# Meta values in four column groups, a reordered last expert, and one activation table for both kinds of head

## What is computed

```python
# first block: 16 meta tokens stand before the 256, so L = 272
xn = rmsnorm(h, norm_mix_g)
sq, sk, sv, dq, dk, dv = split(xn @ w_in)          # 8 heads each
# stick-breaking head (width 128), causal
z = q @ k.T * 128**-0.5
u = where(causal, log_sigmoid(-z), 0)
a = where(causal, exp(log_sigmoid(z) + reverse_cumsum(u) - u), 0);  o = a @ v
# differential head: two softmaxes (width 64 each) with a distance bias
w = p[0] - lam * p[1];  o = rmsnorm(w @ v) * 0.8
h = h + (g0 * (o_sb @ w_br_sb) + g1 * (o_df @ w_br_df)) @ w_out
h = h + swiglu(rmsnorm(h))                          # width 2816
# second block: retention and dilated attention, then 32 experts, 4 a token
u = xb @ w1[e] + b1[e];  a = clamped_swiglu(u);  y += gate * (a @ w2[e] + b2[e])
out = rms_norm(h + modulation * y) * g_final
```

## Time and profile before

| | |
|---|---|
| median of 3 runs | 1876.97 us (1876.14 to 1877.78) |
| profiled execution | 1878.5 us, its span (first to last instruction) 1876.5 us |
| PE busy | 1807.3 us, 96% |
| DVE busy | 816.2 us, 43% |
| ACT busy | 532.4 us, 28% |
| DMA | 568.86 MB, mean 303 GB/s |
| L1136, low parts of the first block's weights | 88 on DVE, 1223 ns each |
| L2181 and L2222, products of the experts | 2048 and 1024 passes on PE, about 595 ns each |

### The profile page before, as it was taken

The page is one execution under the profiler, slowest core; times in us unless marked ns, Lnnn a source line. Parts: engine busy times, 40 slices in busy tenths (PEclk is TensorE's granted clock), DMA queues, the critical chain, the costliest instruction groups (busy, mean ns, idle before and its releaser), DMA issues.

```text
span 1876.5 us, 27470 instructions
## 1 busy us (share of the span) xinstructions
PE 1807.3 (96%) x11187; PEld 1221.8 (65%) x11188; DVE 816.2 (43%) x1363; ACT 532.4 (28%) x860; POOL 39.4 (2%) x65
## 2 busy tenths in 40 slices
PE   7999999999998999999999999999999999999996
PEld 6888889999997899899843443443443434434342
DVE  5445667788884544547522331232221322223222
ACT  5666666434433444455300000000000000000001
POOL 2000000000000000000000000000000000000000
PEclk9999999999997999999999999999999999999998
DMA  7333346778782744435999999999999999999994
GB/s 249 110 111 113 117 131 230 242 234 275 271 309 75 245 159 153 157 127 172 328 428 427 429 426 429 430 427 428 430 427 428 429 428 428 429 429 428 428 429 181
DMA packets 147898, 568.86 MB, mean 303 GB/s; under 512 B 6064, under 2 KB 102424, under 8 KB 123120
## 3 DMA queue, kind: packets, MB, share of 16 engines
q1 hardware_dynamic: 139616, 536.60, 72.5%
q0 software_dynamic: 8208, 31.20, 4.7%
HBM read 566.71 MB, written 3.43 MB: 304 GB/s over the span
## 4 chain that ended last, share of the span: by engine, by line
PE 75%; DMA 18%; DVE 3%; ACT 3%; issue 1%; SPq 0%; DVEq 0%; ACTq 0%
DMA s_ring<-in_w_mlp 17%; PE banks L2181 16%; PE banks L1756 9%; PE banks L2222 9%; PE banks L1758 8%; PE banks L1757 8%; PE banks L2192 4%; PE banks L1911 3%; PE banks L1912 3%; PE banks L1913 3%; PE banks L2165 2%; PE banks L1714 1%; PE banks L1777 1%; DMA s_ring<-in_w_ada 1%; PE banks L2200 1%
## 5 line engine op out<-in xcount | busy, mean ns | idle before, releaser
L2181 PE MATMUL banks<-s_ring,s_W 128*64 128x512 f32 x1568 | 351.6, 596 | 16.9 <-DMA s_ring<-in_w_mlp 15.9
L2181 PEld LDWEIGHTS banks<-s_ring,s_W 128*64 128x64 f32 x1568 | 107.0, 137 | 245.0 <-issue 201.8
L1072 ACT ACTIVATE s_W<-s_W 128x512 f32<-128x512 f32 x32 | 20.1, 630 | 759.7 <-DVE s_W L1624 759.7
L1616 DVE TENSOR_TENSOR s_W<-banks,s_W 128x512 f32<-128x512 f32 x32 | 22.1, 692 | 429.2 <-PE banks L2222 429.2
L2222 PE MATMUL banks<-s_ring,s_W 128*64 128x512 f32 x736 | 161.8, 592 | 0.0
L1366 DVE TENSOR_TENSOR r_w2l<-s_ring,r_w2h 128x1024 fp32r<-128x1024 f32 x96 | 117.3, 1224 | 89.1 <-ACT r_w2h L921 88.9
L1136 DVE TENSOR_TENSOR r_w2l<-s_ring,r_w2h 128x1024 fp32r<-128x1024 f32 x88 | 107.5, 1223 | 92.1 <-ACT r_w2h L737 91.9
L1598 DVE TENSOR_TENSOR s_W<-banks,s_W 128x512 f32<-128x512 f32 x128 | 82.2, 684 | 139.1 <-PE banks L2165 139.1
L1756 PE MATMUL banks<-r_x2h,r_w2h 128*128 128x256 f32 x448 | 131.0, 292 | 5.2 <-DVE r_x2l L1382 5.2
L2192 PEld LDWEIGHTS banks<-s_W 128*128 128x128 f32 x1024 | 116.7, 192 | 24.4 <-issue 24.4
L1758 PE MATMUL banks<-r_x2h,r_w2l 128*128 128x256 f32 x448 | 127.7, 285 | 0.0
(11 more groups left out here) (433 smaller groups left out, 3387.0 us busy)
## 6 DMA issues: line engine op xcount, KB each, us to landing
s_ring<-in_w_mlp SPq DMA_DIRECT2D x144, 2048.0 KB, 30.8
s_W<-in_w_mlp SPq DMA_DIRECT2D x48, 2048.0 KB, 31.0
s_ring<-in_w_in SPq DMA_DIRECT2D x62, 1024.0 KB, 5.1
s_ring<-in_w_ada POOLq DMA_DIRECT2D x24, 1024.0 KB, 9.0
s_ring<-in_w_ffn_gate SPq DMA_DIRECT2D x11, 1024.0 KB, 5.5
s_ring<-in_w_ffn_up SPq DMA_DIRECT2D x11, 1024.0 KB, 10.6
s_ring<-in_w_ffn_down SPq DMA_DIRECT2D x5, 2048.0 KB, 10.2
s_ring<-in_w_gate SPq DMA_DIRECT2D x8, 1024.0 KB, 5.7
```

The lines of the kernel that those rows point to most:

```text
L2181: last = mm(pb[b][64 * h:64 * h + 64, :], XgT[:, 2 * c + k, :], piece(n, 2)[:, k, 1024 * h + 512 * b:1024 * h + 512 * b + 512], start=Fals ...
```

## The change

**Meta values.** xm becomes plain float32: the 16 tokens and 16 columns of zeros. Eight float32 products of the raw weights, one for each block k, go to four groups of 32 output rows (k % 4), so that bank rows 0 to 127 hold four partial sums with zeros between; nothing adds them up but the heads' own products, which now run over all 128 rows (sv[:, 2], dv[:, 2], la, wT), with wvM holding the meta weights eight times. The group moves from the value piece's four units to the start of the unit ahead of it (units 7, 19, 31 and 43). Since DVE overwrites the raw weights, low1 of the piece's first unit waits for the group, and DVE does the low parts of the piece's first three units in that slot (lows1).

**Full rows.** ntriM is 128 rows, zero but for the first 16. L1832, L1844, L1883, L1870 and L1871 lose their narrow shapes.

**Table.** load_log_exp moves from differential head 0 to the start, behind the square root of the token norms.

**Last expert.** The pieces of expert 31 come in the order up 0 to 3, down 0, 1 of expert 30, and then the two of expert 31, the last one in two transfers with semaphores of their own. PE does the four up pieces in a row, the down pieces, with the transposes of expert 31's activation between the two; the last scatter goes to banks 0 and 1. g_final is spread ahead of the last expert and kept in SBUF by ACT (gfin). ACT squares each half of acc when it is complete.

```diff
-GR1, GR2 = group_list(PIECES1), group_list(PIECES2)
 V_KINDS = ("sv", "dv", "rv", "av")
+def meta_first(groups):
+    out = []
+    for x in groups:
+        if x[1] in V_KINDS and x[2] == 0:
+            out.insert(len(out) - 1, x)
+        else:
+            out.append(x)
+    return out
+GR1, GR2 = meta_first(group_list(PIECES1)), group_list(PIECES2)
...
+LAST = (0, 1, 4, 5, 2, 3)
...
+META_OF = {}
+for _n in range(3, len(UNITS1), 4):
+    if PIECES1[_n // 4][0] in V_KINDS:
+        META_OF[_n - 3] = UNITS1[_n].pop(0)
+        UNITS1[_n - 4].insert(0, META_OF[_n - 3])
+def lows1(h):
+    if h + 1 in META_OF:
+        return [h + 1, h + 2, h + 3]
+    return [] if h + 2 in META_OF or h + 3 in META_OF else [h + 3]
...
-    xm = rounded("xm", False, 23168, KT, 2 * M)
+    xm = area(W, 23168, KT, 2 * M)
...
-    skM, ntriM, wvM = area(W, 20864, HEADS, P), W[0:M, 21888:22016], area(W, 22016, 2, 2 * M)
+    skM, ntriM, wvM = area(W, 20864, HEADS, P), W[:, 21888:22016], area(W, 22016, 2, P)
...
+    gfin = W[:, 10368:11392]
...
-        "sc_mm", "acc_done",
-        "over_in", "over_pe", "over_act", "over_dve", "round", "final_sum", "fin_sq", "fin_kept")}
+        "sc_mm", "acc_done", "last_in",
+        "over_in", "over_pe", "over_act", "over_dve", "round", "fin_sq", "fin_kept")}
...
-            n = {0: 0, 1: 1, 4: 2, 5: 3}[p] if e == 0 else 6 * e - 2 + p
+            n = {0: 0, 1: 1, 4: 2, 5: 3}[p] if e == 0 else 6 * e - 2 + (LAST.index(p) if e == E - 1 else p)
...
-        for n in range(176, 6 * E):
+        for n in range(176, 6 * E - 1):
             sp.wait_ge(S["used"], n - 7)
             e, p = (n + 2) // 6, (n + 2) % 6
-            load(n % 8, E if n >= 6 * E - 2 else e, 2 + n % 2 if n >= 6 * E - 2 else p)
+            if n == 6 * E - 2:
+                e, p = E, 2
+            elif e == E - 1:
+                p = LAST[p]
+            load(n % 8, e, p)
+        sp.wait_ge(S["used"], 6 * E - 8)
+        rows = w2[E - 1, 512:1024, :].rearrange("(p k) n -> p k n", p=P)
+        sp.dma_start(piece(7, 4)[:, 0:2, :], rows[:, 0:2, :]).then_inc(inw[7], 16)
+        sp.dma_start(piece(7, 4)[:, 2:4, :], rows[:, 2:4, :]).then_inc(S["last_in"], 16)
...
+        load_log_exp(act)
...
-                rows, at = (2 * M, 2) if n == 0 else (P, n - 1)
-                dst, src, scale = buf[0:rows, at, 512 * part:512 * part + 512], src[0:rows, :], 1.0
+                at = 2 if n == 0 else n - 1
+                dst, scale = buf[:, at, 512 * part:512 * part + 512], 1.0
...
-                if h == 0:
-                    load_log_exp(act)
...
-        with act.Fori(2, E) as e:
+        with act.Fori(2, E - 1) as e:
             expert(e, True, True)
+        for b in range(2):
+            act.wait_ge(S["spread"], b + 3)
+            act.activation(gfin[:, 512 * b:512 * b + 512], pb[4 + b], ACT.Copy).then_inc(S["spread_kept"], 1)
+        expert(E - 1, True, True)
...
+            act.wait_ge(S["over_dve"], n * 8 + 8)
...
-        act.wait_ge(S["final_sum"], 1)
         for t in range(2):
+            act.wait_ge(S["acc_done"], 2 * E - 1 + t)
...
+                if n // 4 * 4 in META_OF:
+                    dve.wait_ge(S["gemm1"], META_OF[n // 4 * 4] + 1)
...
-                meta = wv[:, 0:288].rearrange("p (a n) -> p a n", a=2)[:, :, 0:M].unsqueeze(2).broadcast_to([P, 2, 2, M])
-                nc.vector.tensor_copy(wvM.rearrange("p a (b n) -> p a b n", b=2), meta).then_inc(S["df_w"], 1)
+                meta = wv[:, 0:288].rearrange("p (a n) -> p a n", a=2)[:, :, 0:M].unsqueeze(2).broadcast_to([P, 2, KT, M])
+                nc.vector.tensor_copy(wvM.rearrange("p a (b n) -> p a b n", b=KT), meta).then_inc(S["df_w"], 1)
...
-        st.do(nc.vector.tensor_copy(ntriM.rearrange("p (a n) -> p a n", a=KT), ntri[0:M, 0:M].unsqueeze(1).broadcast_to([M, KT, M])))
+        st.do(nc.vector.memset(ntriM, 0.0))
+        st.wait()
+        st.do(nc.vector.tensor_copy(ntriM[0:M, :].rearrange("p (a n) -> p a n", a=KT), ntri[0:M, 0:M].unsqueeze(1).broadcast_to([M, KT, M])))
         for s, h in ORDER1:
             if s == "G":
-                low1(h + 3)
+                for n in lows1(h):
+                    low1(n)
...
-            if prev:
-                dve.wait_ge(S["used"], 6 * E if isinstance(e, int) and e == E else e * 6 + 2)
+            final, late = isinstance(e, int) and e == E, isinstance(e, int) and e == E - 1
+            def weighed():
+                dve.wait_ge(S["used"], 6 * E if final else e * 6 + (4 if late else 2))
...
+            if prev and not late:
+                weighed()
             if cur:
 
-                dve.wait_ge(S["used"], e * 6 + 4)
+                dve.wait_ge(S["used"], e * 6 + (2 if late else 4))
...
-            if prev:
-                add_up(1, e * 2)
+            if prev and not late:
+                add_up(1, e * 2, 0 if final else 6)
             if cur:
-                choose_b(e + 1)
+                if not late:
+                    choose_b(e + 1)
...
+            if prev and late:
+                weighed()
+                add_up(1, e * 2)
...
-        dve.sem_inc(S["final_sum"], 1)
-        dve.wait_ge(S["spread"], 4)
+        dve.wait_ge(S["spread_kept"], 4)
...
-            stt(otok[:, t, :].rearrange("p (a n) -> p a n", a=2), acc[:, t, :].rearrange("p (a n) -> p a n", a=2), tr[:, t:t + 1],
-                banks[:, 4:6, :], ALU.mult, ALU.mult).then_inc(S["fin_kept"], 1)
+            stt(otok[:, t, :], acc[:, t, :], tr[:, t:t + 1], gfin, ALU.mult, ALU.mult).then_inc(S["fin_kept"], 1)
...
+        def meta_values(g, n):
+            for m in (n // 2, n // 2 + 1):
+                pe.wait_ge(in2[m % 4], 16 * (m // 4 + 1))
+            pe.wait_ge(S["xn_hi"], KT + 2)
+            pe.wait_ge(S["xn_lo"], KT + 2)
+            bank_free(GR1, g, ("act_evac1", "dve_evac1"))
+            for k in range(KT):
+                rows = slice(2 * M * (k % 4), 2 * M * (k % 4) + 2 * M)
+                last = mm(pb[g % 3][rows, :], xm[:, k, :], unit1(raw2, n + k // 2)[:, k % 2, :], start=k < 4, stop=k >= 4, skip_group_check=True)
+            last.then_inc(S["gemm1"], 1)
...
+                if GR1[g][1] in V_KINDS:
+                    meta_values(g, n + 1)
+                    continue
...
-                mm(pb[6][:, 0:T], ntriM, sp[0:M, 384:640], start=True, stop=False)
+                mm(pb[6][:, 0:T], ntriM, sp[:, 384:640], start=True, stop=False)
...
-                tr(pb[6][0:2 * M, 0:P], wvM[:, 0, :], ident)
-                tr(pb[6][0:2 * M, P:T], wvM[:, 1, :], ident).then_inc(S["df_tr"], 1)
+                tr(pb[6][:, 0:P], wvM[:, 0, :], ident)
+                tr(pb[6][:, P:T], wvM[:, 1, :], ident).then_inc(S["df_tr"], 1)
...
-        def scatter(r, n):
+        def scatter(r, n, bank=6):
...
-                last = mm(pb[6 + h], selT[v, P * r:P * r + P], yv[v, :], start=True, stop=True)
+                last = mm(pb[bank + h], selT[v, P * r:P * r + P], yv[v, :], start=True, stop=True)
...
+        def turn(e):
+            since(pe, "a_done", e)
+            since(pe, "at", e - 1)
+            for j in range(4):
+                last = nc.tensor.transpose(pb[4][:, P * j:P * j + P], aa[:, P * j:P * j + P], ident)
+            last.then_inc(S["at_mm"], 1)
+            since(pe, "selg", e)
+            since(pe, "selt", e - 1)
+            for t in range(2):
+                last = nc.tensor.transpose(pb[5][:, P * t:P * t + P], selG[:, t, :], ident)
+            last.then_inc(S["selt_mm"], 1)
+        def down2(at, c, n):
+            n, count = piece_at(at, n)
+            pe.wait_ge(inw[n], count)
+            for k in range(4):
+                if at == E and c == 1 and k == 2:
+                    pe.wait_ge(S["last_in"], 16)
+                for h in range(2):
+                    last = mm(pb[2][64 * h:64 * h + 64, :], aT[:, k, 64 * c:64 * c + 64], piece(n, 4)[:, k, 512 * h:512 * h + 512],
+                              start=c == 0 and k == 0, stop=c == 1 and k == 3, skip_group_check=True)
+            last.then_inc(S["used"], 1)
         def expert(e, cur, prev, at=None):
             at = e if at is None else at
+            final, late = isinstance(e, int) and e == E, isinstance(e, int) and e == E - 1
...
-            if prev:
+            if prev and not final:
                 if isinstance(e, int) and e == 1:
                     pe.wait_ge(S["acc_init"], 4)
-                since(pe, "a_done", e)
-                since(pe, "at", e - 1)
-                for j in range(4):
-                    last = nc.tensor.transpose(pb[4][:, P * j:P * j + P], aa[:, P * j:P * j + P], ident)
-                last.then_inc(S["at_mm"], 1)
-                since(pe, "selg", e)
-                since(pe, "selt", e - 1)
-                for t in range(2):
-                    last = nc.tensor.transpose(pb[5][:, P * t:P * t + P], selG[:, t, :], ident)
-                last.then_inc(S["selt_mm"], 1)
+                if late:
+                    pe.wait_ge(S["spread_kept"], 4)
```

(35 more changed lines are left out.)

29 lines of the change are left out of this document (10 added, 19 removed).

## The result

| | before | after |
|---|---|---|
| median, runs of the comparison | 1876.56 us (4 runs, 1875.98 to 1877.78) | 1851.22 us (4 runs, 1850.89 to 1855.74) |
| profiled execution / its span | 1878.5 / 1876.5 us | 1850.95 / 1849.0 us |
| mean granted clock of the span | 0.988 | 0.993 |
| table loads on ACT | 30 | 13 |

The ratio is 0.987, 95% interval 0.9853 to 0.9887: faster by 25.3 us. 1855.5 was predicted, with a range from 1851.0 to 1863.5; the result lies at the range's lower edge. Between the two profiled executions the gain is 27.5 us where 21.5 were summed up.

A forecast was written before the change was run, and what follows sets the result against it. TensorE bounds the first block, DMA the experts. Meta values -6.8, full rows -9.6, waits +2.1, start +1.0, end -8.2 sum to -21.5 us: 1857.0 from the profiled 1878.5, 1855.5 as median; range 1851 to 1863.5.

The forecast's parts named there:

- Bound and direction: TensorE bounds the first block, the weights' stream the experts; the unedited middle passes the first block's saving on whole.
- Meta values, 2.1 us a piece: First block's value pieces: four column groups run together, 8.4 us for four pieces, a gain of 6.8 us.
- Rival 1: Meta values: only two column groups run at a time, 7.6 us of the gain gone, 1863 us; chance 0.15.
- Full rows, 0.40 each: sbB, sbC and dfC of eight heads: no entering and leaving of narrow tiling, 24 x 0.40 = 9.6 us off TensorE.
- Waits, 3.5 to 5.6: TensorE's idle time before sbB (2.7 to 1.0) and dfB (0.8 to 4.6) in the first block: 2.1 us lost.
- Start, +1.0: Table load right after L724 delays the copy that TensorE's first transposes wait for: 1.0 us lost.
- First block in all, -13.3: First block's terms together: meta values -6.8, full rows -9.6, waits +2.1, start +1.0 us.
- Between the blocks, 0: Middle is not edited and starts when the first block ends, so no gain or loss of its own.
- End, 8.2: Last expert and tail: down products end 3.1 us earlier, the tail behind them 5.1 shorter; bounds 4.5 and 9.
- rival 4: Clock falls again behind expert 30's scatters, where TensorE stands still twice: 2 to 3 us, 1858 us; chance 0.07.
- Rival 2: First block's chains swallow more: DVE's differences late, longer waits before dfB, 5 to 6 us, 1861 us; chance 0.10.
- rivals 3 and 5: 3: compiler inserts table loads, 6 us, 1861, chance 0.02; 5: column groups neither overlap nor change free, 1888, chance 0.02.

The follow-up runs named there:

- the steps earlier: Changed kernel with meta running sums (sbM) at 0 for 1 and differential meta-weight transposes (dfW) at 0.9 for 1.6 in the step list: 1849.20 us, ratio 0.9859.
- the load later: Changed kernel with the first load of the common table behind the first normalisation's work, not right behind L724: 1851.05 us, ratio 0.9866.

## Why the prediction was right, and where not

**Bound and direction: right.** TensorE bounds the first block and the weights' stream the experts, and what the first block saved showed at the feed-forward part's start. That the middle passes it on whole did not hold; see below.

**Meta values, 2.1 us a piece: right** (2.05), from the start of a pair in the earlier trace rows taken over to four groups. Rival 1, at 0.15, would have cost 7.6; with two groups it did cost 6.8. The strict first in, first out of the Trainium skill ("TensorE: Matmul & The Clock Gate", Part 3) is not what these runs show between column groups: four start within 0.02 us, and within 0.04 when each has four passes ahead of the next group's. By the rule read strictly the piece would have taken about 3.5 us (an estimate: 8 steps of the 0.43 us between a group's passes).

**Full rows, 0.40 each: right where it was read, 9.6 us in all somewhat high.** 0.40 in both places shown, and the same again when they were made narrow; but three of the 24 places gave 0.19, which makes 8.6.

**Waits, 3.5 to 5.6: the size was off.** The terms were 1.0 before sbB (0.9 measured) and 4.6 before dfB (2.9 measured); all in all they went from 3.5 to 3.8. I gave heads 1, 4, 5 and 6 waits of 0.3 to 0.4 us; they show 0, 0, 0.13 and 0.14, and 1.31 in head 0 for 1.75. I had also taken these waits for the chains' own length, which the moved steps disproved. That DVE's three differences in one slot cost nothing held: no idle time stands before the value products.

**Start, +1.0: somewhat low.** The transposes came 1.5 later. 1.0 is the load, as costed, and the load moved back brought it back; 0.5 is L762's own lateness, which I did not trace and which differs between executions. Within the first unit's products TensorE then stands still for 1.1 us, waiting for DVE's L1187, which isn't so in every run of the variants; but it had its full clock at 18.4 us for 21.4 before, and the second transposes come 1.3 later (23.75 for 22.42).

**First block in all, -13.3: measured -14.2.** The terms as measured nearly give it: 7.0 (meta values), 8.6 (rows), less 0.3 (waits) and 1.3 (start), are 14.0.

**Between the blocks, 0: this is the step that failed.** I wrote that the middle is not edited and passes the gain on, and allowed 2 us for the clock's steps, at the start only. The middle gave 4.8 us, with 27.3 us at half before and 17.1 after. It is luck and not a merit of the change: the order of a loop without any effect on the work before moved the same stretch by 3.8 us, and two experiments lost there most or all of what they had gained (the steps earlier, the load later). The rows to suspect stood in the trace of before as well: the same 72 passes of one column in the same stretch.

**End, 8.2: measured 7.5.** The tail behind the down products is 5.4 shorter (forecast 5.1). The down products end 7.0 us behind the last landing, where I had 5.9: rival 4, the clock behind expert 30's scatters, at 0.07, came true in the profiled execution, at 1.5 us where I had 2 to 3; where the clock stayed up it was 5.4 to 5.6.

Rival 2 fell with waits of 3.8 us in place of 5.6 or more, rivals 3 and 5 with the 13 table loads and the 0.13 us a pass. The surplus over the forecast, 27.5 - 21.5 = 6.0 us, is 4.8 between the blocks, 0.9 in the first block and 1.0 more until the last landing, less 0.7 at the end. By the medians the surplus is 4.3 us (1855.5 less 1851.22), since the profiled execution of the kernel before had been 1.5 above its median.

## What to carry to other kernels

Before pricing a gain in one engine, look at the chain that engine waits for: the same edit was worth 6.8 us of the first block with the table loads in the chain and 11.1 (15.6 less 4.5) without them. Read the granted clock not only where TensorE is idle, but where it is busy with products of one column: here they cost as much as products of 128 columns (0.108 and 0.112 us a pass) and did not hold the clock up, so write more columns than you need if that is free. What lies between one and 128 columns was not tried. And compare variants by the starts of the same work: a total moved by 4 us through where the clock's steps fell.

## What the runs showed that I had not expected

- 72 passes of one column, 8.5 us in three rows in which TensorE is not idle, cost the clock: a form that writes 128 columns at 0.112 us a pass for 0.108 made the stretch between feed-forward start and second block 7.8 us shorter.
- A gain of 5.8 us can shrink to 1.5 in a stretch that nobody edited, since the clock's steps don't move with the work: two kernels whose work is at the same place up to 356 us have them at 550.9, 561.2 and 571.4, and at 552.0, 558.8 and 575.9.
- A wait costs more than the idle time shown. Moving the steps took 3.6 us of idle time away and won 5.0 behind the second transposes, and the table alone took 2.7 away and won 4.5: the last product before a wait is recorded at 0.28 us where its step is 0.12, so each waiting head loses some 0.16 us that count as busy, and a head can lose up to that and show no idle time. Eight such heads make 1.3 of the table's 1.8 us, so it is not all of the difference; the rest I did not trace.
